# Convolution passes moved behind the value projection of their step, and the second block's means moved to the head of the next step

## The chip, the cores and the metric

The kernel runs on all 8 cores of one Trainium2 chip, as one launch. Each core computes one prompt sequence of 2048 positions and 16 of the 128 sample requests (4 new positions each), so that a core has 2112 columns. No core waits for another. The time is that of the slowest core, in microseconds (us) on the device.

## The reference, cut to what matters

Two layers, each on `x` of width 1024:

```
h   = rmsnorm(x)
p   = h @ w_in                      # 7 parts of 1024: a, g, zA, B, C, hb, zB
u   = a * sigmoid(g)                # group A, 8 heads of 128 channels
ca  = causal depthwise conv of u, width 31, + bias
ca  = layernorm of ca over the 128 channels of the head
yA  = silu(ca * gain + bias) * silu(zA)
v   = C * hb                        # group B, 8 groups of 128 channels
yB  = B * (causal depthwise conv of v, width 3) * silu(zB)
x   = x + concat(yA, yB) @ w_out
```

and an rmsnorm at the end. The last rows of `u` and `v` are outputs too. The sample requests bring 30 and 2 older rows for the two convolutions.

## The kernel before, in words

The 2112 columns of a core are cut into five blocks b = 0 to 4 (four of 424 columns, one of 352 prompt and 64 sample columns). Channels lie on the 128 partitions. A layer first runs group A, as a loop over heads j = 0 to 7 and inside it over the blocks: `a_step` is one step. Then it runs group B, `b_step`, in the same double loop. The output projection, `out_block` (32 matmuls for a block), is run for four finished heads at a time: in group A it stands behind the steps b = 1 to 4 of head 4 and behind step 0 of head 5.

One `a_step` issues, in this order: the gate projection (8 matmuls, L332 by `proj`), its tanh on ScalarE (`a_th`, L606), the value projection (8 matmuls), u on VectorE (`a_u`, L620, with four or eight transfers on SP's queue that copy u in shifted form into `rep`, L594), the gate path's projection (8 matmuls) and its silu on ScalarE (`a_sz`, L634). In the text these are the g, v and z projection.

The wide convolution of a head is not part of its step. It runs on TensorE from `rep`, for two blocks at once, some steps later, through the stages `st_...`; blocks 0 and 1 make one group, 2 and 3 the second, and block 4 a group alone (the single one). `pipe(at, b)` is called at four points of a step (0: at its head; 1: behind the g projection; 2: behind the v projection; 3: behind the z projection) and issues what is due there:

- step 3 runs the convolution of blocks 0 and 1 of the same head, step 0 that of blocks 2 and 3 of the head before, step 2 that of block 4 of the head before (`q_conv[0]["at"] == b`).
- `st_conv`: 32 matmuls of 32 rows of output (L455) into two PSUM banks, and then two copies on VectorE from PSUM to `cb` in bf16, one for each bank (L460, the casts).
- `st_mean`: two matmuls for each of the two blocks (L474) that read both halves of `cb` and take away the mean over the channels, and a Square on ScalarE for each block (L482). The single group has four matmuls and one more for the samples (L477).
- one step later `st_var_mm` (one matmul for each block), `st_rstd` (Ln and Exp on ScalarE, L502 and L503), `st_tt` on VectorE (L509), `st_silu` on ScalarE (L516), and, in the step behind that, `st_y` on VectorE (L523).

Ln and Exp on one side and tanh and silu on the other want different function tables, so ScalarE loads tables twice in every step that has `st_rstd` (steps 1 and 4).

Each engine runs its instructions in the order in which the program issues them. `P.op` notes what an operation reads and writes, and works out from that the semaphores for which it waits; the order on an engine is that of the calls and nothing sorts it. In step 0 VectorE's order before the change is: the two casts of the convolution, the two `st_y` that were put off from step 4, `st_tt` of the single group, u of this step, and then `st_y` of the single group. TensorE's order is g projection, convolution, v projection, mean 0, z projection, mean 1.

The first step of group B's loop (head 0 of `b_step`) still carries the last groups of group A through the same `pipe`.

Of the kernel before, what the change touches and what calls it, by code (L numbers as in the profile page):

```python
# [146 lines left out]
def build_nc():  # L147
# [39 lines left out]
    rep = sb("rep", [128, NR, NT, RW], BF16)  # L187
# [257 lines left out]
    def st_conv(gp, banks):  # L445
        ms, rp, n = gp["j"] % 2, gp["rep"], gp["n"]
        gp["bd"] = banks
        for h in range(2):
            def fn(e, h=h):
                ins = None  # L450
                for m in range(NM):
                    for q in range(4):
                        t = 4 * h + q
                        off = 4 * (NM - 1 - m)
                        ins = e.matmul(psum[32 * q:32 * q + 32, banks[h], 0:n], lhsT=wc[:, ms, NM * t + m, :], rhs=rep[:, rp, t, off:off + n],  # L455
                                       start=(m == 0), stop=(m == NM - 1), tile_position=(0, 32 * q), skip_group_check=True)
                return ins
            P.op("pe", fn, reads=[wc_r[ms], rep_r[rp]], writes=[bank_r[banks[h]]])
        for h in range(2):
            P.op("dve", (lambda e, h=h: e.tensor_copy(cb[:, h, 0:n], bank(banks[h], n))), reads=[bank_r[banks[h]]], writes=[cb_r[h]])  # L460
        for i, s in enumerate(gp["sts"]):
            s["bd"] = banks[i]

    def st_mean(gp, i):
        s, n = gp["sts"][i], gp["n"]
# [60 lines left out]
    q_conv, q_y, hold = [], [], []  # L526
    cur = {}

    def pipe(at, b, alone=True, hook=None):
        single = [cur["s"]] if "s" in cur else []  # L530
        tail = b == 3 and single and not q_conv and "g" not in cur
        if at == 0:
            if tail:
                st_var_mm(single[0], 7)
                st_rstd([], single)
        elif at == 1:
            if b == 3 and single and not tail:
                st_var_mm(single[0], 7)
            if b in (1, 4) and "g" in cur:
                pair = cur["g"]["sts"]  # L540
                for i, s in enumerate(pair):
                    st_var_mm(s, ((1, 7) if b == 1 and alone else (6, 7) if b == 1 else (2, 3))[i])
                st_rstd(pair, [])
                if b == 4 and single:
                    st_rstd([], single)
            if q_conv and q_conv[0]["at"] == b:
                cur["g"] = q_conv.pop(0)
                st_conv(cur["g"], (6, 7) if b == 2 else (4, 5))
            if b % 2 == 0:
                while q_y:  # L550
                    st_y(q_y.pop(0))
            if hook is not None:
                hook()
            if b == 0 and single:
                st_tt(single[0])
                st_silu(single[0])
        elif at == 2:
            if b in (0, 2, 3) and "g" in cur:
                st_mean(cur["g"], 0)
                if b == 2:  # L560
                    cur["s"] = cur.pop("g")["sts"][0]
            if b in (1, 4) and "g" in cur:
                for s in cur["g"]["sts"]:
                    st_tt(s)
            if tail:
                st_tt(single[0])
        else:
            if b in (0, 3) and "g" in cur:
                st_mean(cur["g"], 1)
            if b == 0 and single:  # L570
                st_y(cur.pop("s"))
            if b in (1, 4) and "g" in cur:
                for s in cur.pop("g")["sts"]:
                    st_silu(s)
                    q_y.append(s)
            if tail:
                st_silu(single[0])
                q_y.append(cur.pop("s"))
# [30 lines left out]
    def a_u(st):  # L609
        j, b, ith, bv = st["j"], st["b"], st["th"], st["banks"][1]  # L610
        n = BLOCKS[b][1]
        q0 = HP + BW * (b // 2)
        last = b == NB - 1
        npr = NPL if last else n

        def glu(out, c, d, writes):
            i0, i1 = th_t[:, ith, c:d], psum[:, bv, c:d]
            if len(out.shape) == 3:
                i0, i1 = [v.rearrange("r (p q) -> r p q", p=2) for v in (i0, i1)]
            P.op("dve", (lambda e: e.scalar_tensor_tensor(out=out, in0=i0, scalar=1.0, in1=i1, op0=ALU.add, op1=ALU.mult)),  # L620
                 reads=[bank_r[bv], th_r[ith]], writes=writes)
        glu(ubuf[:, :, q0:q0 + HQ] if last else ubuf[:, b % 2, q0:q0 + n], 0, npr, [u_r[b]])
        if last:
            hw = (WA - 1) // 2
            glu(usam[:, UHN:USW], npr, n, [us_r])
            glu(oa_t[:, j, 0:hw], HQ - hw, HQ, [oa_r[j]])
            glu(oa_t[:, j, hw:], npr - hw, n, [oa_r[j]])
        a_copy(st)
# [13 lines left out]
    def a_step(st, pipe, by_k=False):  # L642
        b, g = st["b"], st["g"]
        sg, sv, szw = st["slots"]
        bg, bv, bz = st["banks"]
        pipe(0, b)
        proj(sg, b, bg, by_k)
        a_th(st)
        pipe(1, b)
        proj(sv, b, bv)  # L650
        a_u(st)
        pipe(2, b)
        proj(szw, b, bz)
        a_sz(st)
        pipe(3, b)
        if b == NB - 1:
            w_free(3)
            a_samp(st["j"], 0)
            w_load(2)
            a_samp(st["j"], 1)  # L660
            if st["j"] + 1 < 8:
                a_hist_load(st["l"], st["j"] + 1)
        else:
            if b == 2:
                w_load((0, 2, 3, 3, 2, 3, 3, 3)[st["j"]], gate=[u_r[2]])
# [49 lines left out]
    def b_step(l, j, b, slots, g=None, mid=None):  # L715
# [19 lines left out]
        else:  # L735
# [2 lines left out]
        P.op("dve", (lambda e: e.tensor_tensor(out=sz_t[:, isz, 0:n], in0=bank(bgb, n), in1=sz_t[:, isz, 0:n], op=ALU.mult)),  # L738
             reads=[bank_r[bgb], sz_r[isz]], writes=[sz_r[isz]])
        if g is not None:  # L740
            pipe(2, b)
        if b_pend and b_pend[0][2] % 2:
            b_flush()
# [40 lines left out]
    def first_head():  # L784
        slots = w_get(3)
        sts = [a_state(0, 0, b, slots) for b in range(NB)]
        for b in range(NB - 1):
            sts[b]["banks"] = (0, 1, 2) if b % 2 == 0 else (3, 4, 5)
        sg, sv, szw = slots

        def stats(b):
            rs_of[b] = rms_stats(b, 6 + b % 2)

        def gproj(b):
            proj(sg, b, sts[b]["banks"][0], True)

        def vz(b):
            proj(sv, b, sts[b]["banks"][1])
            proj(szw, b, sts[b]["banks"][2])

        def evac(b):
            a_th(sts[b])
            a_u(sts[b])
            a_sz(sts[b])

        stats(0)
        P.op("act", lambda e: e.dma_start(out=cw_a[:], in_=cw_a_d[:, 0]), writes=[cwa_r], chan=ch_c[2])
        P.op("act", lambda e: e.dma_start(out=cw_b[:], in_=cw_b_d), writes=[cwb_r], chan=ch_c[3])
        P.op("pe", (lambda e: e.matmul(psum[:, 7, 0:16], lhsT=cmat[:, 0:128], rhs=vecs[:, 16:32], start=True, stop=True)),
             reads=[cmat_r, vecs_r], writes=[bank_r[7]])  # L810
        P.op("act", (lambda e: e.activation(out=cbias[:], in_=psum[:, 7, 0:16], func=AF.Copy)),
             reads=[bank_r[7]], writes=[cbias_r])
        rms_apply(0, 0, rs_of[0])
        gproj(0)
        stats(1)
        rms_apply(0, 1, rs_of[1])
        vz(0)
        stats(2)
        rms_apply(0, 2, rs_of[2])
        gproj(1)  # L820
        vz(1)
        evac(0)
        evac(1)
        P.op("dve", (lambda e: e.tensor_scalar_mul(out=cmat16[:], in0=cmat[:, 0:128], scalar1=0.5)), reads=[cmat_r], writes=[cm16_r])
        a_head_prep(0, 0)
        stats(3)
        rms_apply(0, 3, rs_of[3])
        gproj(2)
        vz(2)
        stats(4)  # L830
        evac(2)
        rms_apply(0, 4, rs_of[4], range(4))
        gproj(3)
        vz(3)
        a_hist_load(0, 0)
        evac(3)
        w_load(1, gate=[u_r[3]])

        def pipe4(at, b):
            if at == 0:  # L840
                first.append(q_conv.pop(0))
                st_conv(first[0], (6, 7))
                rms_apply(0, 4, rs_of[4], range(4, 8))
                a_hist(0, 0)
            elif at in (1, 2):
                st_mean(first[0], at - 1)
            else:
                for i, s in enumerate(first[0]["sts"]):
                    st_var_mm(s, 4 + i)
                st_rstd(first[0]["sts"], [])  # L850
                a_head_prep(0, 1)

        a_step(sts[NB - 1], pipe4, by_k=True)
# [218 lines left out]
```

How the kernel before makes its waits and increments, by code:

```python
            def body(e):  # L119
                waited = {}
                for o in self.ops[eng_name]:
                    need = {}
                    for d in o.deps:
                        s = chan_sems[d.chan] if d.chan is not None else sems[d.eng]
                        if need.get(s.num, (None, 0))[1] < d.cnt:
                            need[s.num] = (s, d.cnt)
                    for num, (s, c) in need.items():
                        if waited.get(num, 0) < c:
                            e.wait_ge(s, c)
                            waited[num] = c
                    ins = o.fn(e)
                    if o.chan is not None:
                        ins.then_inc(chan_sems[o.chan], 16)
                    elif o.sig:
                        ins.then_inc(sems[eng_name], 1)
                if eng_name == "sp":
                    for ch in final_waits:
                        e.wait_ge(chan_sems[ch], chan_total[ch])
```

## Time and profile before

| | |
|---|---|
| median of 3 runs | 1271.69 us (1271.34 to 1273.74) |
| the profiled execution | 1272.57 us |
| its span, slowest core | 1271.0 us (core 3) |
| spans of the other cores | 1261.6 to 1267.7 us |
| TensorE busy | 1188.4 us, 94% |
| VectorE busy | 770.9 us, 61% |
| ScalarE busy | 512.5 us, 40% |
| GpSimd busy | 249.1 us, 20% |
| mean granted TensorE clock, cores 0 to 7 | 0.988 to 0.994 |

The span runs from the first to the last instruction of a core. The busy share of an engine is a mean over stages that differ; group A's loop of the first layer lies between about 60 and 305 us, that of the second between about 660 and 915 us. All rows below are of core 3.

### The profile page before, as it was taken

Reading aid. Unit: us, or ns where it says so; the run is one execution under the profiler, and the core shown is the slowest. Engines: PE = TensorE matmul, PEld = TensorE weight load, DVE = VectorE, ACT = ScalarE, POOL = GpSimd, SP = SyncE. Lnnn points to the kernel's source line nnn. Section 1 sums busy time; section 2 is a strip of 40 time slices with the busy share of each in tenths; the row PEclk is TensorE's granted clock in tenths of the full one; section 3 lists DMA queues with packets and bytes.
Section 4 is the critical chain, followed back from the end, with each engine's and each line's share of the span. In section 5 each row is a group of like instructions: output and inputs, shape, how many; then the busy total and the mean of one; then the engine's idle time right before and its main releaser. Section 6 shows DMA issues by size and latency. Waiting matters only on the chain.

```text
span 1271.0 us, 23082 instructions; the slowest of 8 cores (1261.6 to 1271.0 us)
## 1 busy us (share of the span) xinstructions
PE 1188.4 (94%) x7706; PEld 630.2 (50%) x7706; DVE 770.9 (61%) x1462; ACT 512.5 (40%) x820; POOL 249.1 (20%) x349
## 2 busy tenths in 40 slices
PE   4899999999999999999889999999999999999985
PEld 1345554554555555554435555455545554555542
DVE  3555466544666666675864556645477657665677
ACT  4667743676321101112446675357632110111154
POOL 0044423244010000000003433314411000000002
PEclk9899999999999999999989999999999999999998
DMA  9777753586154114221236775246623221322128
GB/s 240 161 106 125 118 84 67 85 131 111 22 92 71 34 18 104 34 35 34 31 47 102 131 133 94 53 88 124 106 36 53 48 34 18 50 35 34 18 77 206
DMA packets 98756, 101.27 MB, mean 80 GB/s; under 512 B 34448, under 2 KB 79760, under 8 KB 98576
## 3 DMA queue, kind: packets, MB, share of 16 engines
q1 hardware_dynamic: 76800, 57.56, 23.6%
q0 software_dynamic: 20880, 37.89, 19.1%
q10 hardware_dynamic: 960, 4.34, 1.3%
q8 instruction: 65, 1.06, 0.4%
q14 instruction: 51, 0.42, 0.1%
HBM read 92.93 MB, written 13.37 MB: 84 GB/s over the span
## 4 chain that ended last, share of the span: by engine, by line
PE 72%; DMA 8%; ACT 6%; DVE 5%; issue 4%; SPq 3%; POOL 1%; DVEq 0%; ACTq 0%; POOLq 0%
PE ps L332 65%; DMA rep<-ubuf 6%; PE ps L455 3%; ACT sq L351 2%; SPq L594 2%; DMA x_sb<-xT 1%; PE ps L474 1%; PE ps L340 1%; SPq L284 1%; ACT L502 1%; DVE acc L709 1%; DVE ubuf L620 1%; DVE x_sb L406 1%; PE ps L358 1%; ACT rstd_t L502 1%
## 5 line engine op out<-in xcount | busy, mean ns | idle before, releaser
L332 PE MATMUL ps<-h_sb,wsl 128*128 128x424 bf16 (+1 forms) x4400 | 818.6, 342 | 0.1
L332 PEld LDWEIGHTS ps<-h_sb,wsl 128*128 128x128 bf16 x4400 | 426.0, 98 | 359.2 <-issue 13.6
L332 PE MATMUL ps<-y_sb,wsl 128*128 128x424 bf16 (+1 forms) x1280 | 238.8, 345 | 18.8 <-DVE sz_t L738 5.4
L406 DVE TENSOR_TENSOR x_sb<-x_sb,ps 128x424 f32<-128x424 f32 (+1 forms) x320 | 179.0, 592 | 41.8 <-PE ps L332 26.1
L332 PEld LDWEIGHTS ps<-y_sb,wsl 128*128 128x128 bf16 x1280 | 124.6, 98 | 129.2 <-issue 31.0
L314 POOL DMA_DIRECT2D wsl<-w_in_r x112 | 60.9, 548 | 540.6 <-PE ps L332 470.9
L750 ACT ACTIVATE th_t<-ps 128x424 f32<-128x424 f32 (+1 forms) x80 | 41.8, 523 | 237.6 <-PE ps L332 206.2
L731 ACT ACTIVATE sz_t<-ps 128x424 f32<-128x424 f32 (+1 forms) x80 | 41.9, 523 | 219.7 <-PE ps L332 202.8
L709 DVE SCALAR_TENSOR_TENSOR acc<-ubuf,cw_b_sb,acc 128x424 f32<-128x424 bf16 (+2 forms) x176 | 106.6, 606 | 18.4
L620 DVE SCALAR_TENSOR_TENSOR ubuf<-th_t,ps 128x424 bf16<-128x424 f32 (+1 forms) x80 | 46.2, 579 | 109.7 <-PE ps L332 89.5
L433 POOL TENSOR_TENSOR sq<-usam,hista 128x992 f32<-128x992 bf16 x32 | 60.9, 1902 | 217.0 <-DVE oa_t L620 210.3
L761 DVE TENSOR_TENSOR ubuf<-ps,th_t 128x424 bf16<-128x424 f32 (+1 forms) x80 | 46.5, 581 | 78.5 <-PE ps L332 78.5
L738 DVE TENSOR_TENSOR sz_t<-ps,sz_t 128x424 f32<-128x424 f32 (+1 forms) x80 | 47.6, 595 | 75.7 <-PE ps L332 54.4
L439 POOL TENSOR_TENSOR sq<-sq 128x480 f32<-128x480 f32 (+3 forms) x128 | 89.5, 699 | 18.9 <-POOL sq L439 0.9
L460 DVE CAST cb<-ps 128x424 bf16<-128x424 f32 (+1 forms) x96 | 48.4, 513 | 68.7 <-PE ps L455 65.7
L606 ACT ACTIVATE th_t<-ps 128x424 f32<-128x424 f32 (+1 forms) x80 | 41.5, 519 | 87.2 <-PE ps L332 78.7
L523 DVE TENSOR_TENSOR y_sb<-tt_t,sz_t 128x424 bf16<-128x424 f32 (+1 forms) x80 | 61.2, 776 | 23.3 <-ACT tt_t L516 22.3
L455 PE MATMUL ps<-rep,wc 128*32 128x424 bf16 (+1 forms) x1536 | 64.7, 309 | 8.7 <-DMA rep<-ubuf 7.6
L482 ACT ACTIVATE d<-ps,cbias 128x424 bf16<-128x424 f32 (+1 forms) x80 | 48.6, 607 | 55.8 <-PE ps L474 51.4
L509 DVE SCALAR_TENSOR_TENSOR tt_t<-ps,cbias,rstd_t 128x424 f32<-128x424 f32 (+1 forms) x80 | 52.3, 655 | 26.7 <-ACT rstd_t L503 26.7
L358 PE MATMUL ps<-sq,ones_s 128*128 128x424 bf16 (+1 forms) x120 | 34.0, 380 | 34.4 <-ACT sq L351 34.1
L376 DVE SCALAR_TENSOR_TENSOR h_sb<-x_sb,vecs_sb,rstd_t 128x424 bf16<-128x424 f32 (+1 forms) x80 | 47.6, 655 | 29.2 <-ACT rstd_t L369 29.2
(52 smaller groups left out, 735.6 us busy)
## 6 DMA issues: line engine op xcount, KB each, us to landing
wsl<-w_in_r POOLq DMA_DIRECT2D x112, 256.0 KB, 5.4
rep<-ubuf SPq DMA_DIRECT2D x256, 109.0 KB, 5.0
wsl<-w_out_r POOLq DMA_DIRECT2D x32, 256.0 KB, 4.8
x_sb<-xT SPq DMA_DIRECT2D x16, 424.0 KB, 13.9
y_fm<-x_sb SPq DMA_DIRECT2D x16, 424.0 KB, 5.0
rep<-ubuf SPq DMA_DIRECT2D x128, 47.0 KB, 2.3
hista<-hist_a SPq DMA_DIRECT2D x16, 255.5 KB, 4.5
oa_copy<-sa_orig ACTq DMA_DIRECT2D x2, 1664.0 KB, 13.3
```

Of the source, the lines that this page charges most:

```text
L314: P.op("pool", (lambda e, i=i, s=s: e.dma_start(out=wsl[:, s, :], in_=wseq[i])), reads=list(gate), writes=[w_r[s]], chan=ch_w[s], name=f"w ...
L332: ins = e.matmul(bank(bk, n), lhsT=l_, rhs=r_, start=(i == 0), stop=(i == len(pairs) - 1))
L406: P.op("dve", (lambda e, bk=bk, m=m: e.tensor_tensor(out=x_sb[:, m, c0:c0 + n], in0=x_sb[:, m, c0:c0 + n], in1=bank(bk, n), op=ALU.add)), ...
L433: P.op("pool", (lambda e: e.tensor_tensor(out=prod[:, :, :], in0=win(e), in1=hista[:, j % 2, UHN:UHN + WA].unsqueeze(2).broadcast_to([128, ...
L439: P.op("pool", (lambda e, n=n, h=h: e.tensor_tensor(out=prod[:, 0:n - h, :], in0=prod[:, 0:n - h, :], in1=prod[:, h:n, :], op=ALU.add)), r ...
L455: ins = e.matmul(psum[32 * q:32 * q + 32, banks[h], 0:n], lhsT=wc[:, ms, NM * t + m, :], rhs=rep[:, rp, t, off:off + n], start=(m == 0), s ...
L460: P.op("dve", (lambda e, h=h: e.tensor_copy(cb[:, h, 0:n], bank(banks[h], n))), reads=[bank_r[banks[h]]], writes=[cb_r[h]])
L482: P.op("act", (lambda e: e.activation(out=d2[:, i2, 0:nb], in_=bank(bd, nb), func=AF.Square, bias=cbc)), reads=[bank_r[bd], cbias_r], writ ...
L509: P.op("dve", (lambda e: e.scalar_tensor_tensor(out=tt_t[:, it, 0:n], in0=bank(bd, n), scalar=cbc, in1=s["rstd"], op0=ALU.add, op1=ALU.mult)),
L523: P.op("dve", (lambda e: e.tensor_tensor(out=y_sb[:, jj, c0:c0 + n], in0=tt_t[:, it, 0:n], in1=sz_t[:, isz, 0:n], op=ALU.mult)), reads=[tt ...
L620: P.op("dve", (lambda e: e.scalar_tensor_tensor(out=out, in0=i0, scalar=1.0, in1=i1, op0=ALU.add, op1=ALU.mult)), reads=[bank_r[bv], th_r[ ...
L709: P.op("dve", (lambda e, o=o, v=v, wcol=wcol: e.scalar_tensor_tensor(out=o, in0=v, scalar=wcol, in1=o, op0=ALU.mult, op1=ALU.add)), reads= ...
```

## The change: what it does

The convolution's matmuls move from behind the g projection to behind the v projection of the same step (a new call, `pipe(1.5, b)`, ahead of `a_u`). Its casts become a stage of their own, `st_cast`, called at point 2, behind `a_u`. The first mean of a group of two moves from point 2 to point 3, behind the z projection; the second mean moves from point 3 to point 0 of the next step, ahead of its g projection. The single group's means move from point 2 to point 3. In steps 0 and 2 the operation that writes u also waits for the transfers that filled the `rep` of the convolution of this step. The first head of the first layer keeps its order.

```
@@ st_conv
             P.op("pe", fn, reads=[wc_r[ms], rep_r[rp]], writes=[bank_r[banks[h]]])
+        for i, s in enumerate(gp["sts"]):
+            s["bd"] = banks[i]
+
+    def st_cast(gp):
+        banks, n = gp["bd"], gp["n"]
         for h in range(2):
             P.op("dve", (lambda e, h=h: e.tensor_copy(cb[:, h, 0:n], bank(banks[h], n))), reads=[bank_r[banks[h]]], writes=[cb_r[h]])
-        for i, s in enumerate(gp["sts"]):
-            s["bd"] = banks[i]
@@ pipe
             if tail:
                 st_var_mm(single[0], 7)
                 st_rstd([], single)
+            if b in (1, 4) and "g" in cur:
+                st_mean(cur["g"], 1)
         elif at == 1:
...
-            if q_conv and q_conv[0]["at"] == b:
-                cur["g"] = q_conv.pop(0)
-                st_conv(cur["g"], (6, 7) if b == 2 else (4, 5))
             if b % 2 == 0:
                 while q_y:
                     st_y(q_y.pop(0))
...
+        elif at == 1.5:
+            if q_conv and q_conv[0]["at"] == b:
+                cur["g"] = q_conv.pop(0)
+                st_conv(cur["g"], (6, 7) if b == 2 else (4, 5))
         elif at == 2:
-            if b in (0, 2, 3) and "g" in cur:
-                st_mean(cur["g"], 0)
-                if b == 2:
-                    cur["s"] = cur.pop("g")["sts"][0]
             if b in (1, 4) and "g" in cur:
                 for s in cur["g"]["sts"]:
                     st_tt(s)
             if tail:
                 st_tt(single[0])
+            if b in (0, 2, 3) and "g" in cur:
+                st_cast(cur["g"])
         else:
-            if b in (0, 3) and "g" in cur:
-                st_mean(cur["g"], 1)
+            if b in (0, 2, 3) and "g" in cur:
+                st_mean(cur["g"], 0)
+                if b == 2:
+                    cur["s"] = cur.pop("g")["sts"][0]
             if b == 0 and single:
                 st_y(cur.pop("s"))
@@ a_u
-                 reads=[bank_r[bv], th_r[ith]], writes=writes)
+                 reads=[bank_r[bv], th_r[ith]] + passed, writes=writes)
+        passed = [rep_r[cur["g"]["rep"]]] if b in (0, 2) and "g" in cur else []
@@ a_step
         proj(sv, b, bv)
+        pipe(1.5, b)
         a_u(st)
         pipe(2, b)
@@ b_step
         if g is not None:
+            pipe(1.5, b)
             pipe(2, b)
@@ first_head (pipe4)
                 st_conv(first[0], (6, 7))
+                st_cast(first[0])
...
-            else:
+            elif at == 3:
```

## Rows read from the trace of the kernel before

**Rows 1.** The page, part 1: busy us, share of span, instructions.
```profile
PE 1188.4 (94%) x7706; PEld 630.2 (50%) x7706; DVE 770.9 (61%) x1462; ACT 512.5 (40%) x820; POOL 249.1 (20%) x349
```

**Rows 2.** Waits of TensorE over the span: total us, times, longest us.
```profile
PE ps L455 <- DMA rep<-ubuf: 7.6, 9, 1.4
...
PE ps L332 <- ACT sz_t L634: 6.8, 9, 1.9
...
PE ps L474 <- DVE cb L460: 1.7, 2, 0.9
```

**Rows 3.** Timeline of TensorE, second layer, head 6's step 4 on: start, us.
```profile
881.16 4.41 PE L332 MATMUL ps<-h_sb,wsl 128*128 128x416 bf16 x24
885.87 1.62 PE L455 MATMUL ps<-rep,wc 128*32 128x424 bf16 x32 [0.31 <-DMA rep<-ubuf]
887.42 1.61 PE L332 MATMUL ps<-h_sb,wsl 128*128 128x424 bf16 x8
888.87 0.52 PE L474 MATMUL ps<-cb,um_sb 128*128 128x424 bf16 x2
889.23 1.60 PE L332 MATMUL ps<-h_sb,wsl 128*128 128x424 bf16 x8
...
892.46 0.34 PE L332 MATMUL ps<-d,ones_v 128*128 128x424 bf16 x1
...
893.15 4.46 PE L332 MATMUL ps<-h_sb,wsl 128*128 128x424 bf16 x24
897.54 0.79 PE L455 MATMUL ps<-rep,wc 128*32 128x176 bf16 x32
...
904.35 1.62 PE L455 MATMUL ps<-rep,wc 128*32 128x424 bf16 x32 [1.10 <-DMA rep<-ubuf]
```

**Rows 4.** Timeline of VectorE in the same stretch, in head 7's steps 0 and 2.
```profile
886.89 1.32 DVE L460 CAST cb<-ps 128x424 bf16<-128x424 f32 x2 [0.94 <-PE ps L455]
888.78 1.23 DVE L523 TENSOR_TENSOR y_sb<-tt_t,sz_t 128x424 bf16<-128x424 f32 x2 [0.57 <-ACT tt_t L516]
889.93 0.65 DVE L509 SCALAR_TENSOR_TENSOR tt_t<-ps,cbias,rstd_t 128x416 f32<-128x416 f32 x1
890.49 0.59 DVE L620 SCALAR_TENSOR_TENSOR ubuf<-th_t,ps 128x424 bf16<-128x424 f32 x1
...
900.53 0.59 DVE L620 SCALAR_TENSOR_TENSOR ubuf<-th_t,ps 128x424 bf16<-128x424 f32 x1
```

**Rows 5.** Timeline of ScalarE in the same stretch.
```profile
881.11 0.52 ACT L606 ACTIVATE th_t<-ps 128x416 f32<-128x416 f32 x1 [0.52 <-PE ps L332]
...
887.95 1.36 ACT L516 ACTIVATE tt_t<-tt_t,vecs_sb 128x424 f32<-128x424 f32 x2
...
892.21 0.61 ACT L482 ACTIVATE d<-ps,cbias 128x424 bf16<-128x424 f32 x1
892.71 0.53 ACT L606 ACTIVATE th_t<-ps 128x424 f32<-128x424 f32 x1
```

**Rows 6.** Timeline of all engines, first layer, from head 1's step 4 to head 2's step 1.
```profile
94.14 0.52 ACT L606 ACTIVATE th_t<-ps 128x416 f32<-128x416 f32 x1 [0.79 <-PE ps L332]
...
106.21 0.52 PE L332 MATMUL ps<-h_sb,wsl 128*128 128x424 bf16 x2
```

**Rows 7.** Timeline of all engines in group B's head 0, first layer.
```profile
337.82 0.58 DVE L460 CAST cb<-ps 128x176 bf16<-128x176 f32 x2
...
338.66 0.31 PE L474 MATMUL ps<-cb,um_sb 128*128 128x176 bf16 x2 [0.90 <-DVE cb L460]
```

**Rows 8.** Windows: engines' busy us, then the clock granted to TensorE, DMA share, GB/s.
```profile
205.60:209.00 3.40, 1.54 (x10) 0.88 (x10) 1.68 (x4) 3.00 (x4) 2.52 (x5) 1.00 0.28 73
209.00:212.40 3.40, 3.40 (x21) 1.79 (x19) 2.46 (x5) 0.00 (x0) 3.19 (x4) 1.00 0.62 63
653.40:657.40 4.00, 1.64 (x8) 0.49 (x8) 0.59 (x2) 3.66 (x5) 0.00 (x0) 1.00 0.26 72
657.40:660.80 3.40, 3.40 (x11) 1.45 (x11) 0.00 (x0) 2.35 (x3) 0.00 (x0) 0.50 0.79 129
```

## The prediction

> **What bounds the kernel now.** I read the page's busy shares first. TensorE is busy for 94% of the span [rows 1], so an edit counts by what it adds to or takes from TensorE's stops. Next came the list of TensorE's own waits [rows 2]: inside group A's loop they are small. The convolution waits for the shifted copies of u (`rep`) 9 times, 7.6 us together and never over 1.4 us; matmuls wait for the silu of the z path for 6.8 us, and the means for the casts for 1.7 us. Last came the timelines of TensorE, VectorE and ScalarE side by side, over one step 4 and the next head's steps 0 to 2 [rows 3 to 5]. The reader is to see there who is late: TensorE is dense, while ScalarE and VectorE run a long chain that begins with the tanh of step 4 and reaches u of step 0 only when TensorE has gone through the v projection of that step and more.
>
> **What the change removes.** The `rep` waits. Behind the v projection the convolution comes eight matmuls later, 1.45 us (887.42 to 888.87 [rows 3]), and the longest wait was 1.4 us; all nine go. Six of them lie in step 0, three in step 3; the last of these three is 1.10 us and the three make 2.56 us [rows 3]. No instruction is added and none is removed, apart from the waits of u on transfers that the convolution already waits for: u of step 0 ran at 890.49, while the copies were there at 885.87 [rows 3, 4], so that costs nothing. SP's queue gets its transfers behind u as before, in step 3 about one convolution earlier.
>
> **What it moves, on VectorE, step 0.** The casts were first in VectorE's order in step 0; now they stand behind two `st_y`, a `st_tt` and u. These cannot come earlier: the first `st_y` waits for the silu pair of step 4 [rows 4], and that pair stands on ScalarE behind two table loads, six Ln and Exp and a silu. Counted from the tanh of step 4 (881.11) the silu pair starts at 6.84 and u of step 0 at 9.38 [rows 4, 5]. Nothing in this chain moves with the casts, because it waited for ScalarE. In the new order: u starts at 9.38, the first cast at 9.89 and the second at 10.4 (operations ready in a row start about 0.5 us apart; u follows `st_tt` by 0.56 us), the second ends at 11.0, since two casts in a row with gaps take 1.32 us [rows 4]. A mean starts 0.26 us after its last cast (338.40 to 338.66 [rows 7]): mean 0 starts at 11.24.
>
> When is TensorE there? v and z of step 4 and g of step 0 are 24 matmuls from 881.16, three times 1.45 us: until 885.5. Then v 1.45, convolution 1.55 (885.87 to 887.42), z 1.45 [rows 3]: until 889.95, which is 8.84 after the tanh. So TensorE stops for 2.4 us in front of mean 0, where it did not stop before. Behind it come two means (0.36 us each, 888.87 to 889.23), g of step 1 with 1.45 and two variance matmuls of 0.36: v of step 1 starts at 11.24 + 0.72 + 1.45 + 0.36 = 13.77 after the tanh of step 4. Before, it started at 12.04 (893.15 [rows 3]).
>
> Ten heads have this step in full (2, 3, 4, 6 and 7 of both layers). From the tanh of step 4 to v of step 1 they took, in order, 12.07 (the first [rows 6]), 12.76, 12.40, 12.85, 12.03, 12.04, 12.06, 12.33, 12.19 and 12.04 us (the last [rows 3, 5]), 122.8 together with the `rep` and silu waits that they had. New: 137.7. That costs **14.9 us**. The stop is no less than nothing and, were the whole chain 0.3 us later, ten times 2.7; I take 2.4. Head 5 is spared: four times eight output matmuls stand ahead of its step 0, 5.8 us of cover for 2.4. Head 1 of the second layer has no single group (its chain is 1.6 us shorter) and in head 1 of the first layer the order differs; I take 1 us each, **2.0** (0 to 4.8).
>
> **Step 2.** The same pattern, with a shorter chain: the silu pair of step 1, two `st_y`, u, then the casts. The tanh of step 1 starts at 892.71 and u of step 2 at 900.53, 7.82 later [rows 4, 5]. The two casts, of 176 columns, take 0.58 us [rows 7], so mean 0 starts at 7.82 + 0.51 + 0.58 + 0.26 = 9.17. TensorE: the tanh starts 0.25 us behind g's last matmul (892.46 to 892.71 [rows 3, 5]); then two variance matmuls 0.36, v, z and g 4.39 (893.15 to 897.54), v 1.45, convolution 0.72, z 1.45 [rows 3]: 8.12. The stop is 1.05 us. Twelve heads (all from 1 on but head 4's, which has an output block ahead of it): **12.6 us**; between 0, if u comes a microsecond earlier, and 24.
>
> **Step 3** has no such queue: VectorE is free there, the casts follow the convolution, and the z projection covers them. Its three `rep` waits go: **−2.6**. The means next to one another ask more of ScalarE between z and the variances (silu and two Squares of 0.61 [rows 5], about 1.8 us) than TensorE takes for two means and g (2.17): covered, with 0.4 us to spare; without the cover it costs that difference. In group B's head 0 the cast waits (1.7 [rows 2]) go and the second mean, so far behind a transfer's wait, costs 0.36 twice; head 5's output block no longer waits for `st_y` (about 0.8): **−1.8**.
>
> Sum: 14.9 + 2.0 + 12.6 − 2.6 − 1.8 = **25.1 us**.
>
> **The clock.** A stop of 1.86 us left the granted clock at 1.00 (205.60 to 212.40); in the 4 us from 653.40 on, TensorE stood idle for 2.36 us in pieces, and the next 3.4 us were granted 0.50, which is 1.2 of 2.4 GHz [rows 8]. The ten stops of 2.4 us are as long as the second and in one piece like the first. I take a fall at half of them. A fall loses half of 3.4, 1.7 us; a part of that falls on the v and z projections of step 1, where the stop of step 2 swallows it, so 1.4: 5 × 1.4 = **7.0**; bounds 0 and 17.
>
> The Trainium skill (TensorE: Matmul & The Clock Gate, section "HAM oscillation — how this bites in real kernels") tells of a loop in which each tile waits for data and starts at the lower clock after each wait. By that all ten stops would be paid a second time, 17 us in place of 7. The trace agrees with it at 657.40 and not at 209.00.
>
> The profiled execution took 1272.57 us: 1272.57 + 25.1 + 7.0 = 1304.7. It lies 0.9 us above the median of the runs shown, so I predict **1304**.
>
> **The rivals.** (a) *The same stops, no clock falls*: 1272.57 + 25.1 − 0.9 = 1296.8. For it speaks the row of 1.86 us. Chance 0.20. (b) *A clock fall at every stop*: 1296.8 + 17 = 1313.8. For it speaks the row at 657.40; against it, that one stop and a string of stops need not count alike. Chance 0.12. The section of the Trainium skill that is named above is on its side. (c) *ScalarE is late with the second Square*: if the 0.4 us to spare is a wait of 0.5 instead, 14 heads pay 7 us more, 1311. Against it speak the Squares' 0.61 us. Chance 0.08. (d) *Step 2 is covered*: 1296.8 − 12.6 = 1284. Against it: u stood at 7.8 there in all heads that I read. Chance 0.07. (e) *Faster*: the casts do not stop TensorE, and only the removed waits count: 7.6 for `rep`, some 2 of the silu waits, 1.7 for casts: about 11 us, 1261. It decides at u of step 0: if VectorE reaches it 2.4 us earlier than 9.38 after the tanh of step 4, the mean no longer waits. For that the silu pair would have to come earlier, and nothing in the change moves it. Chance 0.05. (f) *No change that can be told* (both sides within 0.2%, about what a measurement of this kernel can tell from no change): the stops eat exactly what the removed waits give. Chance 0.03. My forecast itself has 0.45.
>
> **How the numbers follow.** The range goes from (d) to (b), 1285 to 1315, and leaves out the faster case, the case without a change and the tails of (b) and (c), under 2 in 10. The forecast alone has 1298 to 1310. Slower by over 0.2%: 0.45 + 0.20 + 0.12 + 0.08 + 0.07 = 0.92; same 0.03; faster 0.05.
>
> **What the profile of the changed kernel would show.** TensorE's waits have a new first line in group A: means waiting for casts, 22 to 24 times, some 38 us; the line of `rep` waits is gone or below 1 us. In step 0 u starts 9.4 us after the tanh of step 4 and the casts follow it. In step 3 there is no wait. Granted clock falls to 0.50 behind some of the stops in step 0, so that the mean clock of the cores goes down by about 0.01. The prediction is wrong if the casts of step 0 start before u or if `st_y` comes clearly earlier; wrong in size if the wait for casts stays below 15 us or the variance matmuls get a wait of their own.

## The result, and the profile after

| | before | after |
|---|---|---|
| median on the same chip | 1271.51 us | 1303.78 us |
| ratio after/before, 95% interval | | 1.0243 (1.0216 to 1.0270) |
| profiled execution | 1272.57 us | 1305.07 us |
| span of the slowest core | 1271.0 us | 1303.4 us (core 7) |
| mean span of the 8 cores | 1265.8 us | 1298.0 us |
| mean granted clock, cores 0 to 7 | 0.988 to 0.994 | 0.978 to 0.986 |

The kernel is 31 to 32 us slower. 1304 was forecast. One of the four executions of the changed kernel, 1449.31 us, ran with one die at a lower granted clock (0.83 to 0.85): the ratio leaves such executions out, here and below, while the median of 1303.78 us counts it and is 1302.49 us without it. The rows of after are of core 7, and those of each later run of its slowest core. First the page's shares and two of its groups (busy us, mean ns of one, idle time ahead of them); they answer to [rows 1]:

```profile
PE 1202.3 (92%) x7706; PEld 631.8 (48%) x7706; DVE 761.0 (58%) x1462; ACT 514.7 (39%) x820; POOL 248.9 (19%) x349
...
L477 PE MATMUL ps<-cb,um_sb 128*128 128x424 bf16 (+1 forms) x192 | 39.1, 322 | 33.9 <-DVE cb L465 33.7
...
L455 PE MATMUL ps<-rep,wc 128*32 128x424 bf16 (+1 forms) x1536 | 64.4, 309 | 0.0
```

TensorE runs the same 7706 matmuls. It is busy 13.9 us longer in a span 32.4 us longer. Its waits (total us, times, longest us) show where it now stops:

```profile
PE ps L477 <- DVE cb L465: 33.7, 25, 2.5
...
PE ps L332 <- ACT sz_t L641: 5.3, 4, 1.9
```

Against [rows 2]: the line of `rep` (7.6 us) is gone, and the means' wait for the casts went from 1.7 us to 33.7 us. Of the silu waits 5.3 of 6.8 us are left.

The timelines of three engines, second layer, head 7's step 0, answer to [rows 3 to 5] (start, us; in brackets the idle time ahead and its releaser):

```profile
910.87 5.84 PE L332 MATMUL ps<-h_sb,wsl 128*128 128x416 bf16 x32
916.64 1.62 PE L455 MATMUL ps<-rep,wc 128*32 128x424 bf16 x32
918.19 1.61 PE L332 MATMUL ps<-h_sb,wsl 128*128 128x424 bf16 x8
922.32 1.09 PE L477 MATMUL ps<-cb,um_sb 128*128 128x424 bf16 x4 [2.52 <-DVE cb L465]
923.20 3.03 PE L332 MATMUL ps<-h_sb,wsl 128*128 128x424 bf16 x8
926.03 0.64 PE L332 MATMUL ps<-d,ones_v 128*128 128x424 bf16 x2
926.51 3.75 PE L332 MATMUL ps<-h_sb,wsl 128*128 128x424 bf16 x20
```

```profile
918.50 0.60 DVE L526 TENSOR_TENSOR y_sb<-tt_t,sz_t 128x424 bf16<-128x424 f32 x1 [2.83 <-ACT tt_t L519]
919.50 0.60 DVE L526 TENSOR_TENSOR y_sb<-tt_t,sz_t 128x424 bf16<-128x424 f32 x1 [0.40 <-ACT th_t L612]
920.01 0.64 DVE L512 SCALAR_TENSOR_TENSOR tt_t<-ps,cbias,rstd_t 128x416 f32<-128x416 f32 x1
920.58 0.58 DVE L626 SCALAR_TENSOR_TENSOR ubuf<-th_t,ps 128x424 bf16<-128x424 f32 x1
921.08 1.10 DVE L465 CAST cb<-ps 128x424 bf16<-128x424 f32 x2
```

```profile
910.83 0.52 ACT L612 ACTIVATE th_t<-ps 128x416 f32<-128x416 f32 x1 [0.42 <-PE ps L332]
...
917.66 1.36 ACT L519 ACTIVATE tt_t<-tt_t,vecs_sb 128x424 f32<-128x424 f32 x2
```

The reader is to see the chain that the prediction counted from the tanh of step 4, here at 910.83: silu pair at 6.83 (it was 6.84), u at 9.75 (9.38 was predicted), casts behind u, means at 11.49 (11.24). The convolution ended at about 918.2. Its casts started at 921.08, because four operations stand ahead of them on VectorE: the first `st_y` waits 2.83 us, until ScalarE has the silu pair, the second 0.40 us more, and `st_tt` and u follow without a wait. This is the head with the longest chain; over all ten heads and eight cores the same count gives u at 9.42 and the means at 11.16 in the mean. In this head the clock fell as well: g of step 1 took 3.03 us for eight matmuls in place of 1.60. From the first mean to v of step 1 it is 926.51 − 922.32 = 4.19 us. In head 2 of the first layer, where it did not fall, the same stretch is 107.65 − 105.14 = 2.51 us. Head 3, where it fell again, is between them with 140.57 − 136.70 = 3.87 us:

```profile
105.14 0.88 PE L477 MATMUL ps<-cb,um_sb 128*128 128x424 bf16 x4 [2.10 <-DVE cb L465]
...
107.65 5.90 PE L332 MATMUL ps<-h_sb,wsl 128*128 128x424 bf16 x32
...
116.68 0.46 PE L477 MATMUL ps<-cb,um_sb 128*128 128x176 bf16 x4 [0.87 <-DVE cb L465]
...
123.14 0.88 PE L477 MATMUL ps<-cb,um_sb 128*128 128x424 bf16 x4
...
136.70 0.88 PE L477 MATMUL ps<-cb,um_sb 128*128 128x424 bf16 x4 [2.15 <-DVE cb L465]
...
140.57 6.21 PE L332 MATMUL ps<-h_sb,wsl 128*128 128x424 bf16 x32
```

The rows at 116.68 and 123.14 are the stop of step 2 (0.87 us) and step 3 without a wait. The windows on either side of the step-0 stops at 105.14 and 922.32 answer to [rows 8]; the number behind the five busy times is the granted clock:

```profile
100.80:105.10 4.30, 2.25 (x24) 0.91 (x16) 3.38 (x7) 2.97 (x6) 3.76 (x6) 1.00 0.40 58
105.10:108.60 3.50, 3.46 (x20) 1.94 (x21) 0.87 (x1) 2.15 (x4) 2.96 (x4) 1.00 1.00 182
...
918.20:922.30 4.10, 1.60 (x12) 0.70 (x9) 3.40 (x7) 2.37 (x5) 3.66 (x5) 1.00 0.70 100
922.30:926.50 4.20, 4.18 (x14) 1.91 (x15) 0.54 (x1) 1.35 (x3) 3.19 (x6) 0.59 1.09 190
```

**Where the 32 us are.** The table takes the starts of the variance matmuls, which every kernel has once a group (of a pair the second), as marks, and gives the difference to the kernel before for the stretches between them: the mean over the 8 cores, from one profiled execution of each kernel. "Elsewhere" is what is left of the mean span, in stretches that hardly any kernel edits. It lies between −1.5 and −4.6 us in all columns, so before's own execution was probably rather long there, and single executions differ. Where the second variance matmul comes sooner behind the first, the marks move time from step 0 to step 2: going by the first of a pair, after has 24.7 and 10.4 us in place of 22.7 and 11.8. The same shift puts +0.6 us of head 4's step 2, where nothing stops, into the row of the output blocks (after: −1.1 in head 5's step 0, +0.6 there). The other columns belong to the experiments below.

| us against before | after | s0 | s2 | s3 | means | casts_first | tt_behind | best | y_behind3 | best3 |
|---|---|---|---|---|---|---|---|---|---|---|
| step 0, ten heads | 22.7 | 18.4 | −0.3 | 0.2 | 21.7 | 3.4 | 10.1 | −7.6 | 18.5 | −7.0 |
| step 0, head 1 twice | 1.1 | 1.1 | 0.1 | 0.1 | 1.0 | −0.1 | 1.5 | 0.0 | 3.2 | 0.3 |
| step 2, twelve | 11.8 | 0.2 | 9.7 | 0.0 | 12.0 | 2.2 | 12.4 | 1.9 | 9.0 | 1.6 |
| step 3 | −2.6 | −1.9 | −0.8 | −2.3 | −2.6 | −1.7 | −2.6 | −1.5 | −2.6 | −1.4 |
| output block, heads 4 and 5 | −0.5 | −0.3 | 0.0 | 0.0 | −0.5 | 5.5 | 6.2 | 6.1 | −0.1 | 0.9 |
| group B's head 0 | 1.2 | 3.5 | 0.2 | 2.2 | 0.2 | −0.3 | 2.2 | 0.3 | 3.9 | −0.5 |
| elsewhere | −1.5 | −3.5 | −2.8 | −3.4 | −2.5 | −1.7 | −3.5 | −4.6 | −2.2 | −3.1 |
| mean span | 32.2 | 17.5 | 6.1 | −3.2 | 29.2 | 7.3 | 26.3 | −5.4 | 29.7 | −9.2 |

### The profile page after: what moved, and what is told of

The parts are those of the page before. It is cut to its first block, busy times and chain, and to the rows that moved or that the text cites. A ratio compares the mean times of both kernels' runs of the same rounds, so it can differ in the third digit from the quotient of the medians.

```text
span 1303.4 us, 23046 instructions; the slowest of 8 cores (1295.0 to 1303.4 us)
## 1 busy us (share of the span) xinstructions
PE 1202.3 (92%) x7706; PEld 631.8 (48%) x7706; DVE 761.0 (58%) x1462; ACT 514.7 (39%) x820; POOL 248.9 (19%) x349
## 4 chain that ended last, share of the span: by engine, by line
PE 73%; ACT 8%; DVE 6%; issue 5%; SPq 3%; DMA 3%; POOL 0%; DVEq 0%; ACTq 0%; POOLq 0%
PE ps L332 66%; PE ps L455 3%; PE ps L477 3%; SPq L600 2%; ACT sq L351 2%; DVE cb L465 2%; ACT L505 1%; DMA x_sb<-xT 1%; DMA rep<-ubuf 1%; PE ps L340 1%; SPq L284 1%; DVE ubuf L626 1%; ACT L641 1%; ACT rstd_t L505 1%; ACT tt_t L519 1%
## 5 line engine op out<-in xcount | busy, mean ns | idle before, releaser
L332 PE MATMUL ps<-y_sb,wsl 128*128 128x424 bf16 (+1 forms) x1280 | 242.1, 348 | 17.7 <-ACT sz_t L641 5.3
L739 ACT ACTIVATE sz_t<-ps 128x424 f32<-128x424 f32 (+1 forms) x80 | 41.9, 523 | 219.3 <-PE ps L332 203.4
L526 DVE TENSOR_TENSOR y_sb<-tt_t,sz_t 128x424 bf16<-128x424 f32 (+1 forms) x80 | 56.7, 717 | 57.9 <-ACT tt_t L519 56.9
L641 ACT ACTIVATE sz_t<-ps 128x424 f32<-128x424 f32 (+1 forms) x80 | 41.6, 520 | 95.0 <-PE ps L332 87.6
L477 PE MATMUL ps<-cb,um_sb 128*128 128x424 bf16 (+1 forms) x192 | 39.1, 322 | 33.9 <-DVE cb L465 33.7
```

The lines of the kernel that those rows point to most:

```text
L332: ins = e.matmul(bank(bk, n), lhsT=l_, rhs=r_, start=(i == 0), stop=(i == len(pairs) - 1))
L477: ins = e.matmul(psum[:, bd, c:c + n], lhsT=um[:, 2 * h + p, :], rhs=cb[:, h, 0:n], start=(h == 0 and c == 0), stop=(h == 1), skip_group_c ...
L526: P.op("dve", (lambda e: e.tensor_tensor(out=y_sb[:, jj, c0:c0 + n], in0=tt_t[:, it, 0:n], in1=sz_t[:, isz, 0:n], op=ALU.mult)), reads=[tt ...
L641: P.op("act", (lambda e: e.activation(out=sz_t[:, isz, 0:n], in_=bank(bz, n), func=AF.Silu)), reads=[bank_r[bz]], writes=[sz_r[isz]])
```

## The experiments

My theory: the means wait for casts that stand behind `st_y`, `st_tt` and u on VectorE, in step 0 and step 2, and in step 0 the clock falls behind about half of the stops. Rivals: the stops of one step alone explain the time; the new place of the second mean costs; the clock costs nothing.

**One step at a time (`s0`, `s2`, `s3`).** Steps not named in `LATE` keep the old points for convolution, casts and means (the edit is cut to the convolution and its casts):

```
+    LATE = (0,)          # s0; (2,) in s2; (3,) in s3
@@ pipe, at 1
+            if b not in LATE and q_conv and q_conv[0]["at"] == b:
+                cur["g"] = q_conv.pop(0)
+                st_conv(cur["g"], (6, 7) if b == 2 else (4, 5))
+                st_cast(cur["g"])
```

> Only step 0 in the new order, steps 2 and 3 as before. Theory (the casts wait in VectorE's queue behind two st_y, st_tt and u, which wait for ScalarE): twelve stops of means for casts, ten of them of about 2.1 us as the list of waits counts them, and clock falls behind about half of these; 1293 to 1299 us against 1271.5 before. Rival (the new places of the convolution and the means cost by themselves, alike in each of the three steps): a third of the 32 us, about 1282.

> Only step 2 in the new order. Theory: twelve stops of 0.8 to 0.9 us as the list of waits counts them, none long enough for a clock fall, 11 to 12.5 us, less 1.8 us in group B's head 0: 1280 to 1283 us. Rival (alike in each step): 1282 as well, but with stops that are not put down to the casts.

> Only step 3 in the new order. Theory: VectorE is free in step 3, the z projection covers the casts, and the three rep waits of step 3 (2.6 us) go: 1268 to 1270 us against 1271.5, no wait of a mean for casts but the 1.7 us in group B that were there before. Rival (alike in each step): slower, about 1282.

| | time, us | ratio to before, 95% | means wait for casts | waits for `rep` |
|---|---|---|---|---|
| s0 | 1290.01 | 1.0136 (1.0118 to 1.0153) | 27.0 us, 16 times | 2.5 us, 3 times |
| s2 | 1277.98 | 1.0031 (1.0016 to 1.0045) | 8.2 us, 12 times | 6.6 us, 11 times |
| s3 | 1268.78 | 0.9962 (0.9949 to 0.9976) | 1.8 us, 2 times | 4.9 us, 3 times |

Step 0 and step 2 each cost by themselves, and step 3's part makes the kernel faster, as expected there. `s0` and `s2` came out 3 and 2 us below their ranges. In `s0` the stops are nearly those of after (2.2 us at most), but the granted clock fell behind 18 of the 80 (ten on each of eight cores), where in after it was 42; a fall cost 1.5 us in the mean of those 42, so 24 fewer are 4.6 us on a core. In `s2` a stop took 0.68 us in the mean (8.2 over 12): mean 0 stands 9.14 us behind step 1's tanh there and in after, but TensorE starts the v projection of step 1 0.2 us later behind that tanh and so stops for less. For these two reasons the three ratios, +1.3% together, do not add up to +2.4%. By the table that is 22.7 − 18.4 = 4.3 us in step 0 and 2.1 in step 2; step 3's gain shows in `s0` too (−1.9), where its waits for `rep` fell from 2.4 to 0.7 us, as the mean of the cores, with its order left alone. The rest lies in "elsewhere" and group B, within what single executions differ by, and stays open.

**The place of the second mean (`means`).** Only this is undone:

```
@@ pipe, at 0
-            if b in (1, 4) and "g" in cur:
-                st_mean(cur["g"], 1)
@@ pipe, at 3
                 st_mean(cur["g"], 0)
+                if b != 2:
+                    st_mean(cur["g"], 1)
```

> The changed kernel, but with the second mean of a group of two behind the first at the end of its step instead of at the head of the next one. Theory: what stops TensorE is the first mean's wait for the casts, and the second has them then; no difference beyond 3 us, 1301 to 1307 us, and the waits for casts stay at about 33 us. Rival (the second mean at the head of the next step delays its Square and with it the variance): faster than the changed kernel by 5 us or more, below 1299.

It took 1301.83 us, ratio 1.0223 (1.0207 to 1.0238), with 35.2 us of waits for casts in 26 places. The place of the second mean is worth nothing that these runs can tell; in group A the two means ran back to back either way.

**VectorE's order alone (`casts_first`).** Everything stays where the change put it, but VectorE takes the casts ahead of the two `st_y`, `st_tt` and u; what is added here goes from points 1 and 2:

```
@@ pipe, at 1.5, in group A
                 st_conv(cur["g"], (6, 7) if b == 2 else (4, 5))
+                st_cast(cur["g"])
+                while q_y:                       # with b % 2 == 0
+                    st_y(q_y.pop(0))
+                if b == 0 and single:
+                    st_tt(single[0])
+                    st_silu(single[0])
```

> The changed kernel with VectorE's order of before in group A: the casts directly behind their convolution and ahead of the two st_y, st_tt and u; the convolution and the means keep their new places on TensorE. Theory (the order on VectorE is the cause): the means' waits for casts in group A fall from about 33 us to below 3, no clock falls in group A; ScalarE may now be late with the Squares of step 0, since the single group's silu waits for an st_tt behind the casts: a wait of about 1 us of the variance in ten heads; 1267 to 1275 us in all. Rival (the new places on TensorE cost by themselves): above 1290 us.

It took 1279.84 us, ratio 1.0054 (1.0036 to 1.0072): 1.9 of the 2.4%, about 24 us, come back by the order on one engine, with TensorE's order as in after. That settles the main cause. The last 5 us above the expectation are another thing, which the waits and the timeline of its slowest core show:

```profile
PE ps L332 <- ACT d L485: 12.2, 21, 3.7
...
PE ps L332 <- DVE y_sb L526: 4.1, 2, 2.1
...
218.10 7.47 PE L332 MATMUL ps<-y_sb,wsl 128*128 128x416 bf16 x32 [2.07 <-DVE y_sb L526]
```

The output block of step 0 in head 5 needs the `st_y` of the single group, and that now comes behind casts, two `st_y`, `st_tt` and u. A stop of 2.07 us, and the 32 matmuls behind it took 7.47 us; they take 5.84 to 5.89 us at full clock. The table has 5.5 us for it. And the variance matmuls wait for the Squares (12.2 us in 21 places): about 0.7 us in each of the ten heads, near the 1 us expected, 2.0 us in head 1 of the first layer and, on this core, 3.7 us in head 6 of the second. The expectation that no clock falls in group A was wrong: it fell 21 times on the eight cores, ten of them at head 5's output block and eight in head 1 of the first layer.

**Shortening the stop (`tt_behind`).** One `st_tt` less stands ahead of the casts; the chain is 0.6 us shorter. The single group's silu goes behind the Squares with it, and both means of step 0 stand behind z, which `means` showed to be worth nothing (the edit is cut to `st_tt`):

```
-            if b == 0 and single:
+            if b == 0 and single and not alone:
                 st_tt(single[0])
@@ at 2, behind st_cast
+            if b == 0 and single and alone:
+                st_tt(single[0])
```

> The changed kernel with one operation fewer ahead of the casts in step 0: st_tt of the single group stands behind them, its silu behind both Squares, and both means of step 0 behind the z projection. The stops of step 0 get shorter by one st_tt, 0.56 us, from about 2.1 to 1.6 us as the list of waits counts them. If the clock falls hang on the length of the stop, they vanish in group A's step 0 (stops of 1.9 us did not bring one before), which gives 5.6 us for the stops and about 6 for the clock: 1291 to 1294 us. If the falls come with any stop of this kind, their number stays at about 5 a core and the time is 1297 to 1300 us.

1297.35 us, ratio 1.0200 (1.0184 to 1.0216). By its time it belongs with the reading that the falls stay, and that would be misread. A step-0 stop and what follows it:

```profile
101.73 0.88 PE L477 MATMUL ps<-cb,um_sb 128*128 128x424 bf16 x4 [1.54 <-DVE cb L465]
...
844.35 7.47 PE L332 MATMUL ps<-y_sb,wsl 128*128 128x416 bf16 x32 [2.43 <-DVE y_sb L526]
```

```profile
100.20:101.70 1.50, 0.00 (x0) 0.00 (x0) 1.50 (x4) 0.53 (x1) 1.49 (x3) 1.00 0.88 153
101.70:105.20 3.50, 3.47 (x20) 1.95 (x21) 1.09 (x2) 2.79 (x5) 3.07 (x4) 1.00 1.01 160
```

With stops of 1.53 to 1.91 us the granted clock stayed at 1.00 behind all ten of these step-0 stops, on all 8 cores, and step 0 costs 10.1 us where it cost 22.7. The 6.2 us at head 5 hide part of it: a new stop of 2.43 us ahead of the output block, with a fall in the second layer on all eight cores (the row at 844.35: 32 matmuls in 7.47 us in place of 5.84 to 5.89).

**`st_y` behind the casts (`y_behind`, `y_behind3`).** The two `st_y` move from point 1 to point 2, behind `st_cast`. In `y_behind`, and in `best2` below, the single group's `st_tt` rotates into one of the two `tt` buffers that a put-off `st_y` has still to read, so that yA of one block is not the reference's there and `st_tt` waits for the silu pair. `y_behind3` gives it a buffer of its own, the first half of `acc`, which group A leaves free:

```
+    ttb = [tt_t[:, 0, :], tt_t[:, 1, :], acc[:, 0, :]]
+    def st_tt(s, third=False):
+        s["tt"] = it = 2 if third else rot_tt.next()
@@ pipe, behind st_cast at 2
+            if b % 2 == 0 and alone:
+                while q_y:
+                    st_y(q_y.pop(0))
```

> The changed kernel with the two put-off st_y of steps 0 and 2 moved behind the casts in group A; st_tt and u stay ahead of them. Theory (each operation ahead of the casts holds them until ScalarE lets it go): u is next in line, and its tanh stands on ScalarE behind the silu pair of the step before, so u starts about 8.7 us after the tanh of step 4 in place of 9.4. The stops of step 0 shrink only from 2.1 to about 1.5 us, those of step 2 from 0.9 to about 0.7, and the clock no longer falls in step 0: 1287 to 1293 us. If the two st_y alone were the cause: about 1268 us.

> The changed kernel with the two put-off st_y of steps 0 and 2 moved behind the casts in group A, and a buffer of its own for the single group's st_tt (the first half of acc, which group A does not use), so that st_tt need not wait for the pair whose st_y are put off. Theory: st_tt is early, and what still holds the casts is u, whose tanh stands on ScalarE behind the silu pair; u starts about 8.7 us after the tanh of step 4 in place of 9.4, the stops of step 0 are about 1.5 us, those of step 2 about 0.7 to 0.9, no clock falls in step 0: 1287 to 1293 us. If the two st_y alone were the cause: about 1268 us.

`y_behind` took 1297.25 us, ratio 1.0202 (1.0184 to 1.0221); `y_behind3` 1300.29 us, ratio 1.0219 (1.0195 to 1.0243). Both missed 1287 to 1293. Timelines of `y_behind3`, head 3's step 0, TensorE, then VectorE and ScalarE:

```profile
134.29 0.88 PE L477 MATMUL ps<-cb,um_sb 128*128 128x424 bf16 x4 [1.44 <-DVE cb L465]
...
137.12 0.34 PE L332 MATMUL ps<-d,ones_v 128*128 128x424 bf16 x1 [0.52 <-ACT d L485]
```

```profile
132.53 0.60 DVE L632 SCALAR_TENSOR_TENSOR ubuf<-th_t,ps 128x424 bf16<-128x424 f32 x1 [2.85 <-ACT th_t L618]
133.04 1.10 DVE L465 CAST cb<-ps 128x424 bf16<-128x424 f32 x2
134.06 3.31 DVE L529 TENSOR_TENSOR y_sb<-tt_t,sz_t 128x424 bf16<-128x424 f32 x2
```

```profile
131.91 0.51 ACT L618 ACTIVATE th_t<-ps 128x424 f32<-128x424 f32 x1
...
135.94 0.52 ACT L647 ACTIVATE sz_t<-ps 128x424 f32<-128x424 f32 x1 [2.90 <-DVE y_sb L529]
136.37 1.11 ACT L485 ACTIVATE d<-ps,cbias 128x424 bf16<-128x424 f32 x2
```

The stop shrank to 1.44 us, since u now comes right behind its tanh, and no clock fell in step 0; so far the theory holds. But u waits for a tanh that ScalarE does at 131.91, behind the silu pair: VectorE was not the only engine late. And the two `st_y`, put off, run beside GpSimd's `sq` products and take 3.31 us in place of 1.23 [rows 4]. Until the first of them is done, silu of z may not write its buffer (the wait of 2.90 us), behind it come the Squares, and the variance matmuls wait for those. A new wait took the place of the one that went.

**Versions that keep the good part (`best`, `best2`, `best3`).** All three put the casts ahead of the two `st_y` and u on VectorE in step 0, let both means of step 0 stand behind z, and leave step 0 of group B's head 0 in the old order. They differ in the single group: in `best` its silu stands behind the Squares, in `best2` and `best3` its `st_tt` and silu stay at point 1, in `best3` in the buffer of its own.

```
@@ pipe, at 1.5 (best, best2, best3)
+                if alone:
+                    st_cast(cur["g"])
+            if alone:
+                if b % 2 == 0:
+                    while q_y:
+                        st_y(q_y.pop(0))
@@ best3, at 1
-                st_tt(single[0])
+                st_tt(single[0], alone)
                 st_silu(single[0])
```

> As the kernel with the casts first, and in step 0 both means behind the z projection and the single group's silu behind their Squares; group B's head 0 keeps the old order in its step 0. Theory: neither casts nor Squares stop TensorE, the rep waits and the silu waits of before are gone as well: 1258 to 1264 us, faster than before (1271.5) and than the changed kernel. Rival (the new places on TensorE cost by themselves): above 1290 us. If ScalarE's tables or the Squares bind in step 0 all the same: 1266 to 1272.

> As the kernel called best, but the single group's st_tt stands ahead of the casts, where its operands are there early, and its silu ahead of the silu of this step, as before the change; VectorE's order in step 0 is st_tt, casts, two st_y, u. Theory: the casts are still in time, the Squares are in time, and head 5's output block no longer waits for the single group's st_y (2.4 us and a clock fall, once a layer, in best): about 6 us less than best, 1258 to 1263 us. If the new places on TensorE had a cost of their own that best hides: no faster than best, 1266 us or more.

> VectorE's order in group A's step 0: st_tt of the single group (with a buffer of its own), casts, two st_y, u; in step 2: casts, two st_y, u; both means of step 0 behind its z projection; group B's head 0 with the old order in its step 0. Theory: casts and Squares are in time, and head 5's output block does not wait for the single group's st_y as it did in best: about 6 us less than best, 1258 to 1263 us. If the new places on TensorE had a cost of their own: 1266 us or more.

| | time, us | ratio to before, 95% |
|---|---|---|
| best | 1267.56 | 0.9956 (0.9942 to 0.9971) |
| best2 | 1282.13 | 1.0083 (1.0069 to 1.0097) |
| best3 | 1262.16 | 0.9924 (0.9902 to 0.9947) |

`best` missed its range for the reason seen in `casts_first`: two waits of the output block for `st_y`, 4.9 us, with a fall behind 8 of the 16 on the eight cores. `best2` missed because `st_tt`, in the shared buffer, waits for the silu pair (17.3 us of TensorE's waits for the Squares); `best3` differs from it in that buffer alone and has 3.7 us. `best3` came in as expected, 0.8% faster than before and 3.2% than after (1262.16 over 1303.78). Its head 2, step 0, TensorE and then VectorE:

```profile
98.31 1.62 PE L455 MATMUL ps<-rep,wc 128*32 128x424 bf16 x32 [0.15 <-DVE acc L515]
99.86 1.61 PE L332 MATMUL ps<-h_sb,wsl 128*128 128x424 bf16 x8
101.31 0.88 PE L477 MATMUL ps<-cb,um_sb 128*128 128x424 bf16 x4
102.03 1.60 PE L332 MATMUL ps<-h_sb,wsl 128*128 128x424 bf16 x8
103.46 0.52 PE L332 MATMUL ps<-d,ones_v 128*128 128x424 bf16 x2
103.82 5.90 PE L332 MATMUL ps<-h_sb,wsl 128*128 128x424 bf16 x32
```

```profile
97.49 0.65 DVE L515 SCALAR_TENSOR_TENSOR acc<-ps,cbias,rstd_t 128x416 f32<-128x416 f32 x1 [0.38 <-ACT rstd_t L506]
99.33 1.32 DVE L465 CAST cb<-ps 128x424 bf16<-128x424 f32 x2 [1.19 <-PE ps L455]
100.56 1.10 DVE L529 TENSOR_TENSOR y_sb<-tt_t,sz_t 128x424 bf16<-128x424 f32 x2
101.58 0.59 DVE L645 SCALAR_TENSOR_TENSOR ubuf<-th_t,ps 128x424 bf16<-128x424 f32 x1
```

From the convolution to v of step 1 TensorE has no wait. The casts now wait for TensorE (1.19 us) and not the other way about, and u still starts at 101.58, where nobody was waiting for it.

## Why the prediction was right, and where its steps were off

- **The mechanism** was the forecast one: casts behind u, u behind a chain that begins with step 4's tanh, TensorE stopped ahead of the means. The profile of after shows it (u at 9.42 us in the mean where 9.38 was reckoned, means at 11.16 where 11.24), and `casts_first` shows it by taking it away.
- **Step 0 and the clock**, 14.9 + 7.0 = 21.9 us predicted, 22.7 measured. The lists of waits show stops of 2.09 to 2.17 us (2.52 to 2.54 in head 7 of the second layer), 2.17 in the mean, where the prediction took 2.4. Most of that is the way of counting: a list counts from the modelled end of the last matmul, the prediction from where the next one would have started, and by that the stop is 2.34 us. Half of the stops with a fall, 5 of 10, was a choice between two rows and came out by luck: the runs had 5.25 on a core (42 on eight cores) in after, and 2.25 behind nearly the same stops in `s0`. What a fall costs was put at 1.4: measured 4.19 − 2.51 = 1.68 us in the head shown, 3.87 − 2.51 = 1.36 in head 3 of the first layer, and 1.5 in the mean of the 42. So rivals (a) and (b) are out. `tt_behind` shows how near (a) was: 0.5 us less of a stop, and none falls.
- **Head 1**, 2.0 predicted, 1.1 measured. **Step 2**, 12.6 predicted, 11.8 measured: the stop is 0.87 as shown against 1.05, and where the clock fell it shrinks, to as little as 0.26, as the prediction let it be swallowed. Rival (d) is out. Its price, 1284, lies just under the range of 1285 to 1315 that is said to begin with it.
- **Step 3**, −2.6 predicted and measured. No variance matmul of step 4 waited for a Square in after: rival (c) is out. (In step 0 two did, 0.5 us together, in head 1 of the first layer.) In `y_behind3`, where the Squares of step 0 come later, that wait appears there at once.
- **Rival (e)** was decided at u, and u came no earlier. With the casts ahead of u, the gain that it told of exists (`best3`).
- **The step that was off** is in the term of −1.8: group B's head 0. Head 5's output block gave what was forecast (−1.1 in its step 0, about −0.8 reckoned). Group B's head 0 was put at −1.0 and cost 1.2. The waits of before, 0.90 us [rows 7] and 0.8 in step 2, are gone (the row at 355.75), and that step is 1.9 us shorter. But for step 0 the prediction had only the second mean's 0.72. There the casts stand behind two `st_y`, `st_tt` and a product of group B, and mean 0 now waits for them, 0.66 and 0.72 us. The step became 3.1 us longer, and on seven of eight cores the clock fell once, behind the stop of the output block that follows:

```profile
326.41 0.52 PE L477 MATMUL ps<-cb,um_sb 128*128 128x424 bf16 x2 [0.66 <-DVE cb L465]
328.18 7.58 PE L332 MATMUL ps<-y_sb,wsl 128*128 128x424 bf16 x32 [1.25 <-ACT d L485]
...
355.75 0.46 PE L477 MATMUL ps<-cb,um_sb 128*128 128x176 bf16 x4
...
955.62 0.52 PE L477 MATMUL ps<-cb,um_sb 128*128 128x424 bf16 x2 [0.72 <-DVE cb L465]
```

  How much of the 3.1 us the change makes stays open. `s2` and `s3` leave this step in the old order and have 2.2 and 2.1 us more than before there, with six falls each; before had a stop ahead of the output block too, of 1.2 to 2.1 us, and none.
- This miss of 2.2 us, with 0.8 in step 0, was made up by head 1 (−0.9), step 2 (−0.8) and "elsewhere" (−1.5). So that 1304 lies within 2 us of either median is in part luck: the terms were right to about 2 us each, and "elsewhere" is no term of the prediction.
- **The profile's signs**: 33.7 us in 25 places against some 38 us in 22 to 24; the `rep` line gone (7.6 us on before's slowest core, 5.0 in the mean of its cores); the clock, as the mean of the eight cores, down from 0.991 to 0.983, where about 0.01 was foretold.

## What to carry to other kernels

Before work that TensorE waits for is put behind other work in an engine's queue, write out that queue and ask of each operation ahead of it what it waits for itself; a copy that was ready at once became late by 3 us through neighbours that wait for ScalarE. Here the means moved back and the casts with them, and that cost 31 us; with the means back and the casts left early the kernel gained 0.8% (`best3`). And put off work only after looking up who waits for the buffer that it holds: the put-off `st_y` held the silu of z, and the next stage waited for that.

## What the runs showed of the hardware

- **Stops of about 2.1 us and the clock.** In after the granted clock fell to 0.50, 1.2 of 2.4 GHz, behind 42 of the 80 step-0 stops of 2.09 to 2.54 us; behind those of 1.53 to 1.91 us in `tt_behind` and of 1.43 to 1.73 us in `y_behind3` it fell at none of 80 each, as at 1.86 us before [rows 8]. Length alone does not decide: 2.10 at 105.14 left 1.00 and 2.15 at 136.70 did not, of the eight longest, 2.52 to 2.54 us, three fell, and `s0` with nearly the same stops had 18 falls. Nor is a stop under 1.9 us always free: in group B's head 0 the clock fell behind a stop of 1.25 us that had one of 0.66 us shortly ahead of it (326.41 and 328.18). What decides is not settled here. The Trainium skill (TensorE: Matmul & The Clock Gate, section "HAM oscillation — how this bites in real kernels") gives as its rule a length that gaps of TensorE should not pass, and it is longer than any of these stops. By that none of them would cost the clock, so the section does not stand on the side of rival (b), as the prediction has it; the traces disagree with the rule, with falls behind 2.09 to 2.54 us.
- **VectorE beside GpSimd.** A pair of `st_y`, each with two fp32 inputs in SBUF, took 3.31 us at 134.06 in `y_behind3`, while GpSimd ran its `sq` products, and 1.10 us at 100.56 in `best3`, where it ran none; the pair of casts from PSUM took 1.10 us at 133.04, the second of them with the `sq` product of 133.50 beside it:

```profile
133.50 1.89 POOL L433 TENSOR_TENSOR sq<-usam,hista 128x992 f32<-128x992 bf16 x1
135.53 3.65 POOL L439 TENSOR_TENSOR sq<-sq 128x480 f32<-128x480 f32 x4
```

  The Trainium skill (SBUF — State Buffer, section "Who interferes with whom") says that a VectorE instruction with two SBUF inputs contends with a GpSimd instruction that reads SBUF; these rows agree.
